# Attention outputs in three slots and stored by SyncE, one-bank scores in two banks, first state-space input matrices formed in the last head

## What is computed

```python
h = rmsnorm(x, norm_mix_g[l])
z = h @ w_in[l]
u_pool, u_ssm, q, k, v, logf = split(z)
gates = sigmoid(z[..., COL_GATE:]).reshape(B, L, 3, D_MODEL)
y_a = pool_mixer(u_pool, ...)
y_b = ssm_mixer(u_ssm, s0, lam, log_dt, b, c, ...)
y_c = fox_attention(q, k, v, c_q, c_k, pos)
proj = einsum('blnw,nwd->blnd', stack([y_a, y_b, y_c]), w_branch)
x = x + sum(gates * proj, axis=2) @ w_out
x = x + conv_ffn(rmsnorm(x, norm_ffn_g), ...)
...
# attention: 8 heads x 64, softmax(q k / 8 + c_q - c_k, causal) v
# state space: 32 groups of 16 channels, 64 complex states each
```

## Time and profile before

| what | value |
|---|---|
| median of three runs | 1920.14 us (1918.97 to 1920.38) |
| the profiled execution's own time | 1920.72 us |
| its span | 1919.0 us |
| TensorE busy in the span | 1859.6 us, 97% |
| VectorE, ScalarE, GpSimd busy | 1186.5, 432.2, 808.8 us |
| mean granted TensorE clock | 0.992 |

### The profile page before, as it was taken

How to read it: one execution, slowest core, us unless ns; L and a number is a source line. 1 busy time by engine, 2 the same in 40 slices (tenths; PEclk the granted TensorE clock), 3 DMA queues, 4 the chain that set the end, 5 groups by cost and what they waited for, 6 DMA issues and landing times. The chain is left out here.

```text
span 1919.0 us, 28813 instructions
## 1 busy us (share of the span) xinstructions
PE 1859.6 (97%) x11323; PEld 1803.0 (94%) x11323; DVE 1186.5 (62%) x1820; ACT 432.2 (23%) x812; POOL 808.8 (42%) x461
## 2 busy tenths in 40 slices
PE   7999999989997999999999999999999999999997
PEld 6989999888987989989999999999999999999997
DVE  6688653888874456444573587556556556556556
ACT  4210123555551111140011221111111111111113
POOL 4434344333327456322232355535535535525530
PEclk8999999999998999999999999999999999999999
DMA  8634839664725544256541111111111111111102
GB/s 269 177 129 131 259 117 259 169 169 129 183 70 156 122 94 110 72 173 220 184 172 45 45 55 56 44 33 55 44 33 55 44 33 55 44 33 55 44 23 95
DMA packets 221949, 203.97 MB, mean 106 GB/s; under 512 B 58305, under 2 KB 200621, under 8 KB 221154
## 3 DMA queue, kind: packets, MB, share of 16 engines
q1 hardware_dynamic: 199250, 166.00, 30.3%
q10 hardware_dynamic: 22608, 36.72, 5.7%
HBM read 138.44 MB, written 59.77 MB: 103 GB/s over the span
## 5 line engine op out<-in xcount | busy, mean ns | idle before, releaser
L154 PE MATMUL bank<-act_hi,w_hi 128*128 128x364 f32 (+1 forms) x2544 | 848.1, 333 | 9.4 <-DVE act_lo L1454 3.8
L154 PE MATMUL bank<-act_lo,w_hi 128*128 128x364 f32 (+1 forms) x2544 | 837.7, 329 | 0.0
L154 PE MATMUL bank<-act_hi,w_lo 128*128 128x364 f32 (+1 forms) x2544 | 836.9, 329 | 0.0
L154 PEld LDWEIGHTS bank<-act_hi,w_hi 128*128 128x128 f32 x2544 | 479.6, 189 | 16.6 <-issue 10.8
L154 PEld LDWEIGHTS bank<-act_lo,w_hi 128*128 128x128 f32 x2544 | 479.3, 188 | 1.0 <-issue 0.3
L154 PEld LDWEIGHTS bank<-act_hi,w_lo 128*128 128x128 f32 x2544 | 479.0, 188 | 0.0
L2731 DVE SCALAR_TENSOR_TENSOR conv<-up_raw,cw,conv 128x1090 f32<-128x1090 f32 x86 | 179.9, 2092 | 63.8 <-ACT up_raw L2617 33.5
L2414 POOL CAST w_hi<-w_raw 128x1024 fp32r<-128x1024 f32 x44 | 47.5, 1080 | 356.8 <-PE bank L154 351.7
L154 PE MATMUL bank<-ffn_hi,down_hi 128*128 128x364 f32 (+1 forms) x528 | 174.0, 330 | 0.7 <-DVE up_raw L2765 0.5
L154 PE MATMUL bank<-ffn_lo,down_hi 128*128 128x364 f32 (+1 forms) x528 | 173.0, 328 | 0.0
L154 PE MATMUL bank<-ffn_hi,down_lo 128*128 128x364 f32 (+1 forms) x528 | 172.7, 327 | 0.0
(11 more groups left out here) (302 smaller groups left out, 2461.4 us busy)
## 6 DMA issues: line engine op xcount, KB each, us to landing
w_raw<-in_w_up SPq DMA_DIRECT2D x44, 512.0 KB, 3.8
w_raw<-in_w_in SPq DMA_DIRECT2D x42, 512.0 KB, 4.5
gate<-gate_scratch ACTq DMA_DIRECT2D x24, 544.0 KB, 4.1
w_raw<-in_w_down SPq DMA_DIRECT2D x22, 512.0 KB, 3.3
gate_scratch<-gate_out ACTq DMA_DIRECT2D x48, 182.0 KB, 2.4
w_raw<-in_w_branch SPq DMA_DIRECT2D x12, 512.0 KB, 4.0
kh<-kh_scratch SPq DMA_DIRECT2D x16, 336.0 KB, 7.5
kl<-kl_scratch SPq DMA_DIRECT2D x16, 336.0 KB, 8.5
```

What stands on the lines that cost most here:

```text
L154: mm = pe.matmul(out, w(k), x(k)[:, c0:c0 + cn], start=first and k == ks[0] and n == 0, stop=last and k == ks[-1] and n == 2)
```

## The change

1. The output of attention gets three slots (`out_slot`): the first four groups of a head alternate between slots 0 and 1, the group of 64 queries has slot 2 to itself. Its stores move from ScalarE's queue to SyncE's (`out_store` in `sync`), and SyncE's whole order is written anew: the loads of q, k and terms of head h+1 come when all units of head h-1 are scored and read, those of the values when its last product is done, and the gate tiles each at a place of its own, with the stores in between.
2. One-bank scores use banks 1 and 2 in turn (`score_banks`), and from unit 5 of a head on `score(n)` waits for one unit less (`scores_read`).
3. The first state-space tile's `ssm_w` is formed in the last head (`input_step`, six steps after the masks of n = 64 to 69). Its table and matrices lie where head 6 had its q, k and terms; each head's buffers are therefore allocated apart. The table is loaded once head 6 is scored. `inputs(0)` is gone from the second block, with the table's and one gate tile's load.

```diff
+        def scores_read(n):
+            return n if n % UNITS < 5 else n - 1
+        def out_slot(g):
+            h, i = divmod(g, 5)
+            return (i % 2, 256 * (i % 2), 2 * h + i // 2) if i < 4 else (2, 512, h)
...
+            load_values(sp, 0)
+            load_gate(2)
+            load_qk(sp, 1)
+            load_terms(sp, 1)
+            load_values(sp, 1)
+            load_gate(3)
+            for n in range(N + 3):
+                h, i = divmod(n + 2, UNITS)
+                if i == 0 and 1 <= h <= HEADS - 1:
+                    sp.wait_ge(score_done, UNITS * h)
+                    sp.wait_ge(top_done, UNITS * h)
+                    if h < HEADS - 1:
+                        load_qk(sp, h + 1)
+                        load_terms(sp, h + 1)
+                    else:
+                        sp.dma_start(m.tab[0][:], m.tab_d[:, 0:NB]).then_inc(m.tab_ld[0], 16)
+                if n - 1 in group_of:
+                    out_store(group_of[n - 1])
+                h, i = divmod(n - 2, UNITS)
+                if i == 0 and 1 <= h < HEADS - 1:
+                    sp.wait_ge(pv_done, 5 * h)
+                    load_values(sp, h + 1)
+                if n - 2 in free_at:
+                    load_gate(free_at[n - 2] + 2)
...
+                step = n - (N - UNITS) - 1
+                if 0 <= step < 6:
+                    input_step(pool, m, 0, *divmod(step, 3))
...
-                    pe.wait_ge(top_done, n)
-                banks, cn = score_banks(n)
+                    pe.wait_ge(top_done, scores_read(n))
+                banks, cn, b0 = score_banks(n)
...
-                act.wait_ge(o_st[g % 2], 32 * (g // 2) + 32)
+                act.wait_ge(o_st[a], 32 * count + 32)
...
-                if n >= N:
-                    out_store(group_of[n])
...
-                if n - 1 in group_of and n - 1 < N and n != N:
-                    out_store(group_of[n - 1])
...
         gate_split(12)
-        inputs(0)
         gate_split(13)
         inputs(1)
```

More of the change, by code:

```diff
@@ L71 @@
 class StageSems:
-    FIRST = 128
+    FIRST = 130
     def __init__(self, nc):
@@ L487, in attention_engines @@
         pth, ptl = (x[:, P:].rearrange("p (s b c) -> p s b c", s=2, c=256) for x in (pth_z, ptl_z))
-        oh, ol = sb("o_hi", [HD, 2, 256], F32R), sb("o_lo", [HD, 2, 256], F32R)
+        oh, ol = sb("o_hi", [HD, 512 + TS], F32R), sb("o_lo", [HD, 512 + TS], F32R)
         mask = sb("mask", [P, P])
@@ L570, in first_loads @@
             load_terms(sp, 0)
-        def sync(sp):
[L573 to L593, removed]
@@ new lines, in load_values @@
+        def load_values(sp, h):
+            j, rows = h % 2, slice(h * HD, (h + 1) * HD)
+            for half, src in ((0, m.vh_d), (1, m.vl_d)):
+                dst = vhl[:, :, :, half * HD:(half + 1) * HD].bitcast(F32)
+                by_tile = lambda r0, r1: src[r0:r1, rows].rearrange("(k p) d -> p k d", p=P)
+                sp.dma_start(dst[:, j, 0:8], by_tile(0, TP)).then_inc(v_ld[j], 16)
+                sp.dma_start(dst[0:TS, j, 8], src[TP:T, rows]).then_inc(v_ld[j], 16)
+                sp.dma_start(dst[:, j, 9:11], by_tile(T, TK)).then_inc(v_ld[j], 16)
@@ new lines, in attention_engines, with load_gate, out_store @@
+        free_at = {n: p // 3 + 2 for n, p in piece_of.items() if p % 3 == 2 and p // 3 + 2 <= GATES}
+        def sync(sp):
+            def load_gate(t):
+                sp.wait_ge(ws.w_split, t + 1)
+                sp.dma_start(m.raw[:, t % 2], w[:, :, t * P:(t + 1) * P]).then_inc(ws.raw_ld[t % 2], 16)
+            def out_store(g):
+                h, q, nq, _ = group(g)
+                a, c0, _ = out_slot(g)
+                sp.wait_ge(o_lo, g + 1)
+                for dst, src in ((m.yh_d, oh), (m.yl_d, ol)):
+                    sp.dma_start(dst[2, h * HD:(h + 1) * HD, 256 * q:256 * q + nq],
+                                 src[:, c0:c0 + nq].bitcast(F32)).then_inc(o_st[a], 16)
+            load_values(sp, 0)
[22 more added lines that the diff above has]
+                    load_gate(free_at[n - 2] + 2)
@@ L638, in gpsimd @@
             split_tile(pool, m, ws, 1, 1, by_channel(m.gain1[:]))
-            free_at = {n: p // 3 + 2 for n, p in piece_of.items() if p % 3 == 2}
             for n in range(-2, N):
-                if n + 2 in free_at and free_at[n + 2] <= GATES:
+                if n + 2 in free_at:
                     scale(free_at[n + 2])
@@ L744, in scalar @@
         def scalar(act):
-            for a in range(2):
+            for a in range(3):
                 act.sem_inc(o_st[a], 32)
@@ L1757, in mix_engines @@
     tiles = range(MW)
-    tab_ld, ut_ld = [sem(f"tab_ld{a}") for a in range(2)], [sem(f"ut_ld{t}") for t in tiles]
+    tab, w, tab_ld, ut_ld = m.tab, m.w, m.tab_ld, [sem(f"ut_ld{t}") for t in tiles]
     u2_ld = [sem(f"u2_ld{a}") for a in range(2)]
@@ L1776, in mix_engines @@
         ["y_lo3_3"] + [f"r{o}" for o in tiles] + [f"r_lo{o}" for o in tiles])
-    pool_did = Steps(sem("pool_did"), [f"{n}{t}" for t in tiles for n in ("w_a0", "w_b0", "w0_", "w_a1", "w_b1", "w")])
+    pool_did = m.pool_did
     gate_w = gate_columns(io)
@@ L2942, in build @@
         m.b0_ld = keep("b0_ld")
-        m.o_st, m.g_st = [keep("o_st0"), keep("o_st1")], [keep(f"gate_st{g}") for g in range(3)]
+        m.o_st, m.g_st = [keep(f"o_st{a}") for a in range(3)], [keep(f"gate_st{g}") for g in range(3)]
+        m.tab_ld = [keep("tab_ld0"), keep("tab_ld1")]
+        m.pool_did = Steps(keep("pool_did"), [f"{n}{t}" for t in range(MW) for n in ("w_a0", "w_b0", "w0_", "w_a1", "w_b1", "w")])
         m.piece_mm = keep("piece_mm")
```

115 lines of the change are left out of this document (61 added, 54 removed).

## The result

The changed kernel takes **1900.74 us** (median of four runs: 1898.77, 1899.79, 1901.68 and 6430.94; nothing shows what disturbed the last, and it is left out of the ratio) against 1920.26 beside it: ratio **0.9892** with a 95% interval from 0.9878 to 0.9906. The forecast was 1902.2. The profiled execution took 1899.79, its span 1898.0; so it is 20.9 us shorter than the one before, where the sum of the prediction had 17.9. Of these 20.9 us, 1.8 lie ahead of attention: its first score begins at 309.80 for 311.58.

A forecast was written before the change was run, and what follows sets the result against it. TensorE, busy 97%, was taken as the bound, its gaps and low clock as the gain. From 1920.7, 20.5 us less and 2.6 more gave 1902.8, or 1902.2 from the runs' median; range 1898 to 1906, wider 1896 to 1911.

The forecast's parts named there:

- four rivals: Stores wait in every head (5%); store waits stay (15%); last head slows (12%); second-block wait only moves (8%).
- C: Last head: steps of 4.19 us make the masks late, attention ends 8 us later, 1910 us; chance 12%.
- boundary: wait and clock: Start of second block: TensorE's 8.9 us wait for `ssm_w` and 2.4 us of low clock go, 11.3 us together.
- stores in three slots, clock after them: Attention, change of heads: three `pt_hi` gaps, 6.2 us, and 1.7 us of low clock after the last go.
- scores in two banks: Attention: four small TensorE gaps before the 64-row scores, put down to a bank VectorE reads, go: 1.3 us.
- six steps in the last head: Last head: GpSimd's steps collide with VectorE's `o_lo`, costing 1.5 us, between 0 and 4 us.
- new waits, start: Attention: 1 us of new waits for VectorE, plus 0.1 us for a gate tile loaded later at the start.
- Rival D: Second block: `cl` or the next gate tile ends the wait later, half of 11.3 us won, 1908; chance 8%.
- ScalarE also no longer issues 80 transfers; TensorE doesn't wait for that, so it counts nothing: Attention: taking the store issues off ScalarE was credited with no gain.
- I take the waits to be gone: Attention: ScalarE's waits for `yl_scratch` stores, 13.4 us in four, were expected to vanish or stay under 1 us.
- Rival A: Changes of head: stores behind loads on SyncE's queue hold slots, 34 us where 7.9 is paid, 1935; chance 5%.
- Attention 8 to 10 us shorter: Whole attention block: a sign that the forecast was right, its length falling by 8 to 10 us.

The follow-up runs named there:

- e6: Changed kernel with two output slots again and ScalarE issuing the stores at the old places: 1914.93 us, ratio 0.9970.
- e2: Changed kernel with all one-bank scores in bank 1 again, each score waiting for all earlier units: 1901.91 us, ratio 0.9893.
- e1: Changed kernel with the six input-matrix steps back in the second block: 1902.84 us, ratio 0.9909.
- e3: Changed kernel with ScalarE issuing the output stores at their old places, three slots kept: 1909.99 us, ratio 0.9940.
- e5: Changed kernel with two output slots again, stores still issued by SyncE in the new order: 1906.73 us, ratio 0.9922.
- e4: Changed kernel with all six steps moved behind the last normalisation of attention: 1893.64 us, ratio 0.9859.
- e8: Changed kernel with only the last two of the six steps moved behind the last normalisation of attention: 1896.13 us, ratio 0.9865.

## Why the prediction was right, and where not

The total was right, 1900.7 for 1902.2, and none of the four rivals came about, though the last head did slow down, as C had it. But two terms were off by much more than the total, in opposite directions: that the sum came so close is luck.

| term | predicted | measured |
|---|---|---|
| boundary: wait and clock | -11.3 | -11.4 (from block 2 on) |
| stores in three slots, clock after them | -7.9 | -15.0 (e6) |
| scores in two banks | -1.3 | -0.2 (e2) |
| six steps in the last head | +1.5 | +7.5 (last head: change against e1) |
| new waits, start | +1.1 | the rest, about -2, of which -1.8 ahead of attention |
| sum | -17.9 | -20.9 |

The last column's terms come from different sources (e6 and e2 from medians, the others from single traces), so they fit the sum to a few us only.

**Matrices earlier: right, and for the reason given.** The 8.9 us and the 2.4 us of clock add to 11.3; 11.4 came. Rival D did not occur: `cl` was in time, and the gain was carried to the end.

**"ScalarE also no longer issues 80 transfers; TensorE doesn't wait for that, so it counts nothing": wrong, the largest miss.** Issuing and the wait for `o_lo` ahead of it were worth 9.2 us (e3). I had priced the stores by the one wait with a name, `yl_scratch`, and followed only TensorE's waits of over 1 us. The rows for more were there. VectorE's 27.9 us of waiting for `pt_hi` I called slack; it was the chain by which ScalarE's lateness reached TensorE. After the change it reads:

```profile
DVE pt_lo L904 <- ACT pt_hi L811: 6.0, 13, 0.7
```

And in ScalarE's waits, just above and below the 13.4 us that I took, the kernel before has these, which I left:

```profile
ACT pt_hi L773 <- issue: 16.0, 13, 2.8
...
ACT pt_hi L777 <- issue: 12.0, 6, 3.1
```

What shows the price is windows from head to head, in which the seven heads before the last had 0.8 to 3.5 us each without work for TensorE, and the waits of its weight loads, 23.9 us where the matmuls' own come to 13.7.

**"I take the waits to be gone": right.** The slot did it (e5: four waits, 16.0 us, without it), not the queue. Rival A, SyncE's queue as the new bottleneck, did not occur, but its late stores did. The median store landed 1.9 and 2.1 us after its issue, against 2.3 and 2.5 on ScalarE's queue before; those issued right behind a head's loads of q, k and terms (one in each of five heads, at 382.2, 412.6, 441.5, 471.1 and 500.2 us) took 8.3 to 10.8 us. The Trainium skill (DMA: Bandwidth & Descriptors, section on queues, rings and completion order) has each ring taken in order; these five agree, but on ScalarE's own ring up to 11.0 us were measured as well, so the ring is not the whole reason. The third slot gave them the time.

**"I take 1.5 us" for the last head: mis-sized by 6.** The bound of 4 us rested on `o_lo` as "VectorE's only instruction here with two SBUF inputs". The scaling of `prob` (L879), one tensor and one column, is held in the same way: 2.03 us for 0.35. Secondly I spread the steps evenly over units of 3.8 us; but the last units have 1 to 3 key blocks, are the shortest of all, and the steps push the gate tile's subtraction in beside them (from 24.2 us behind the cut in e4 to 27.2 in the change and e8). Thirdly the clock: I credited its loss where gaps go, and didn't charge it where new gaps could come. Rival C named the place but the wrong engine: steps took 1.98 to 2.66 us, not 4.19, GpSimd was in time with nearly all masks (VectorE waited three times, 4.5 us in all, 3.5 of it once at the start of attention), and it was VectorE that was held, not GpSimd.

**Two claims that were not worked out.** "Attention 8 to 10 us shorter" didn't follow from the sum, which gives 6.6. The second block begins 9.6 us earlier, but 1.8 of that lie ahead of attention, so attention itself is 7.8 us shorter. "Idle time at the barrier down from 20.5 us by the 12.4 us of the steps": it is 19.73, since the steps filled holes inside the head and the end of the head got longer.

**The banks: nothing.** I had priced four gaps of 0.3 us as the wait for a bank. With one bank (e2) the gaps are gone just the same, so VectorE's lateness made them, and the other parts of the change took it away. The term was credited to the wrong part.

## What to carry to other kernels

An engine that issues DMAs pays for them in its own stream (here 1.1 us a pair), the busy share doesn't show it, and what the issue waits for is paid as well. So a wait put down to "issue" just ahead of a link in the chain is a price, not noise; move such issues to an idle queue, above all those that wait for another engine's data. When work is moved onto GpSimd, look at all VectorE instructions beside it that work SBUF to SBUF, not only at those with two inputs, and put it where the bound engine has the longest cover: here six steps behind the last scaling and not among the masks were worth 6.3 us. And compare like stretches (head with head) before believing the waits of TensorE's matmuls alone: they had 8.0 of the 13.4 us that the heads gave, the waits of its weight loads 13.5.

## What was not expected of the hardware

- A scaling on VectorE with one SBUF tensor as input (128x256, 0.35 us alone) took 2.03 us beside GpSimd's subtraction, and 128x128 took 1.32 for 0.29. The Trainium skill (SBUF — State Buffer, section on the two separate sides) names, as users of the port pair shared with GpSimd, VectorE operations in a two-port performance mode beside those with two SBUF inputs. The hold of 1.7 us agrees, and I should have weighed that half of the rule too; that this scaling runs in such a mode is read from its being held, and no run shows it by itself.
- Instructions of the two engines queued back to back take turns: each VectorE instruction ends 0.1 to 0.3 us behind a GpSimd instruction, and GpSimd's own are hardly longer (2.35, 1.98, 2.41 us). In this stretch VectorE pays for both.
- The granted clock doesn't follow the length of a gap alone. Before, a gap of 1.97 us left it at 1.00 from 395 to 405 us. In the changed kernel one of 1.42 us, at 350.68, stands in a stretch at 0.66:

```profile
350.00:355.00 5.00, 4.32 (x18) 4.32 (x19) 3.58 (x11) 1.87 (x4) 0.60 (x2) 0.66 1.00 289
```

The same matmul has the same gap before, and there the clock stays, as it does in e1 and e4:

```profile
353.57 0.45 PE L719 MATMUL bank<-pt_lo,vhl 128*64 128x256 f32 x2 [1.42 <-DVE pt_lo L875]
```

```profile
350.00:355.00 5.00, 3.58 (x23) 2.98 (x22) 4.93 (x10) 1.72 (x6) 3.27 (x3) 1.00 1.05 219
```

So with the same code and the same gap (the change and e1) the clock can fall in one execution and not in another. Here the fall cost 5 x 0.34 = 1.7 us. What decides it stays open.
